# Attention steps of a fused two-block kernel: ScalarE's weight split behind the odd step's copy, TensorE's output-matrix products in front of the odd step's second turning

## The reference, cut to what matters

```
def attend_block(qi):                     # first_block, nsa_mixer
    s = einsum(q, k_cmp) - slope * d_cmp;  p_cmp = masked_softmax(s, d_cmp >= 0);  o_cmp = p_cmp @ v_cmp
    s = einsum(q, k_sel) - slope * d_sel;  p_sel = masked_softmax(s, d_sel >= 0);  o_sel = p_sel @ v_sel
    s = einsum(q, k_win) - slope * d_win;  p_win = masked_softmax(s, m_win);       o_win = p_win @ v_win
    return g[0] * o_cmp + g[1] * o_sel + g[2] * o_win
o = lax.map(attend_block, ...)            # all query blocks, [256, 16 * 64]
return o @ w_out                          # the output matrix, 1024 x 1024
```

## Time and profile before

| what | value |
|---|---|
| median of 3 runs | 2440.98 us (2439.84 to 2443.73) |
| profiled execution: own time | 2448.22 us |
| profiled execution: span of the trace | 2446.4 us |
| mean granted TensorE clock | 0.989 of full |
| PE busy | 2319.2 us (95%) |
| DVE busy | 1764.6 us (72%) |
| ACT busy | 1270.6 us (52%) |
| attention steps in the trace | about 838 to 926 us from the span's start |

### The profile page before, as it was taken

The page is one execution under the profiler, slowest core; times in us unless marked ns, Lnnn a source line. Parts: engine busy times, 40 slices in busy tenths (PEclk is TensorE's granted clock), DMA queues, the critical chain, the costliest instruction groups (busy, mean ns, idle before and its releaser), DMA issues.

```text
span 2446.4 us, 44735 instructions
## 1 busy us (share of the span) xinstructions
PE 2319.2 (95%) x16584; PEld 2055.4 (84%) x16584; DVE 1764.6 (72%) x2815; ACT 1270.6 (52%) x1939; POOL 12.2 (0%) x28
## 2 busy tenths in 40 slices
PE   4999999998999889999999999999999999999998
PEld 4888888888888768888889898888888888988887
DVE  6888978888888677766667575666666675746666
ACT  4445354453545565446446573554464475536544
POOL 0000000000000000000000000000000000000000
PEclk9999999999999999999999999999999999999999
DMA  8886868868898314754555341455555543404653
GB/s 322 303 290 217 292 249 295 291 218 294 301 308 302 104 53 163 240 199 156 191 190 177 129 139 55 155 174 190 190 174 191 189 164 122 147 30 155 200 191 123
DMA packets 130436, 481.39 MB, mean 197 GB/s; under 512 B 14608, under 2 KB 14656, under 8 KB 129776
## 3 DMA queue, kind: packets, MB, share of 16 engines
q1 hardware_dynamic: 128448, 468.36, 56.1%
q0 software_dynamic: 1840, 10.93, 1.2%
HBM read 478.15 MB, written 1.07 MB: 196 GB/s over the span
## 4 chain that ended last, share of the span: by engine, by line
PE 76%; DVE 9%; ACT 8%; issue 5%; DMA 2%; SPq 0%; DVEq 0%; ACTq 0%
PE bank L589 74%; ACT work L1367 2%; ACT w_hi L1367 2%; DMA ring<-weights 2%; DVE w_lo L1975 2%; ACT sq L1367 1%; DVE y L2009 1%; PE bank L620 1%; ACT L1367 1%; ACT h_split L1367 1%; PE bank L1183 0%; DVE work L2355 0%; DVE y L2487 0%; DVE work L2282 0%; DVE y L2123 0%
## 5 line engine op out<-in xcount | busy, mean ns | idle before, releaser
L589 PE MATMUL bank<-h_split,w_hi 128*128 128x256 f32 (+1 forms) x5232 | 1147.1, 341 | 27.2 <-DVE w_lo L1975 10.3
L1975 DVE TENSOR_TENSOR w_lo<-ring,w_hi 128x1024 fp32r<-128x1024 f32 x715 | 871.1, 1223 | 378.9 <-ACT w_hi L1367 378.1
L1367 ACT ACTIVATE w_hi<-ring 128x1024 fp32r<-128x1024 f32 x726 | 765.2, 1057 | 641.5 <-PE bank L589 565.9
L589 PEld LDWEIGHTS bank<-h_split,w_hi 128*128 128x128 f32 x5232 | 894.2, 193 | 124.1 <-issue 22.0
L589 PE MATMUL bank<-h_split,w_lo 128*128 128x256 f32 x3896 | 741.2, 284 | 0.0
L589 PEld LDWEIGHTS bank<-h_split,w_lo 128*128 128x128 f32 x3896 | 611.5, 192 | 25.0
L1367 ACT ACTIVATE work<-bank 128x512 f32<-128x512 f32 (+1 forms) x249 | 146.8, 593 | 322.1 <-PE bank L589 293.5
L589 PE MATMUL bank<-w_hi,act_hi 128*128 128x512 f32 x704 | 275.3, 391 | 0.0
L589 PE MATMUL bank<-w_lo,act_hi 128*128 128x512 f32 x704 | 274.9, 391 | 0.0
L589 PE MATMUL bank<-w_hi,act_lo 128*128 128x512 f32 x704 | 273.9, 389 | 0.0
L2009 DVE CUSTOM_DVE_ANT_0 y<-ring,v_first 128x1024 f32<-128x1024 f32 x160 | 189.6, 1220 | 14.6 <-DMA ring<-weights 14.6
(11 more groups left out here) (217 smaller groups left out, 1570.0 us busy)
## 6 DMA issues: line engine op xcount, KB each, us to landing
ring<-weights SPq DMA_DIRECT2D x886, 512.0 KB, 4.9
work<-cmp POOLq DMA_DIRECT2D x1, 4096.0 KB, 14.7
sq<-rows POOLq DMA_DIRECT2D x6, 512.0 KB, 6.2
work<-lora POOLq DMA_DIRECT2D x2, 1024.0 KB, 5.1
x<-x_in SPq DMA_DIRECT2D x1, 1024.0 KB, 11.1
out<-y SPq DMA_DIRECT2D x2, 512.0 KB, 2.6
const_sb<-consts SPq DMA_DIRECT2D x1, 854.0 KB, 12.7
const_sb<-consts POOLq DMA_DIRECT2D x1, 726.0 KB, 7.2
```

The costliest lines, as they stand in the source:

```text
L589: return nc.tensor.matmul(out, lhsT, rhs, start=start, stop=stop, skip_group_check=skip)
L1367: return nc.scalar.activation(out, in_, f, bias=bias, scale=scale, **kw)
L1975: tt(w_lo[q % SLOTS][:, :], ring[n % RING][:, c * HALF:(c + 1) * HALF], w_hi[q % SLOTS][:, :].bitcast(F32), ALU.subtract).then_inc(halves_ ...
```

## The change

Two edits in the loops over the 16 steps.

On TensorE, the odd step's second turning moves from in front of the previous step's output-matrix products to behind them. On ScalarE, the split of the next weight half (`advance`) moves from behind `exps(s+2)` in step 1 and the even steps 2 to 14, to between `copy(s)` and `exps(s+2)` in the odd steps 1 to 15. Step 0's split stays where it is. The halves split are the same and in the same order. VectorE's, GpSimd's and SyncE's programs are unchanged.

```
--- before.py
+++ after.py
@@ -907,8 +907,6 @@
                     turned_(s, 0)
                     if 0 < s < 14:
                         scores(s + 2)
-                    if s % 2:
-                        turned_(s, 1)
                     if s == 0:
                         pe.wait_ge(*at_vec.at("pc"))
                         for i in range(4):
@@ -917,6 +915,8 @@
                         ins.then_inc(*at_pe.step("cmp_turned"))
                     if s:
                         spread_half(s - 1)
+                    if s % 2:
+                        turned_(s, 1)
                     values(s)
                 spread_half(15)
@@ -1602,14 +1602,14 @@
                     if s:
                         high(s - 1)
                     copy(s)
+                    if s % 2:
+                        advance(st.half + 12 + s // 2)
                     if s < 14:
                         exps(s + 2)
                     if s == 14:
                         root_table()
-                    if s < 2:
-                        advance(st.half + 11 + s)
-                    elif s % 2 == 0:
-                        advance(st.half + 12 + s // 2)
+                    if s == 0:
+                        advance(st.half + 11)
                 high(15)
```

## The result

The changed kernel took 2452.19 us, the median of 6 executions (2450.44 to 2454.53), against 2442.69 us for 6 executions of the kernel before (2439.84 to 2446.42). The ratio is 1.0035, 95% interval 1.0025 to 1.0045: slower by 6 to 11 us. The forecast was 2445.5 us and its range ended at 2448.4. The direction was right and the size wrong: the two medians differ by 9.5 us, where 4.5 was forecast. Later samples say how much of the difference belongs to the change: two further sets of 12 executions of the same changed kernel gave ratios of 1.0016 and 1.0023, that is 4.0 and 6.2 us.

The account below looks back on a forecast made before the run. The prediction took the alternation of ScalarE and VectorE in the attention steps as the bound, with TensorE entering the path after the change. Terms 2.3 + 1.65 + 0.5 = 4.5 us on 2441.0 gave 2445.5 us, range 2442.6 to 2448.4.

Parts of the forecast that it names:

- What bounds the kernel: Attention steps: ScalarE and VectorE wait for each other in turn, 10.0 us per pair; TensorE is near this chain, not in it.
- The split costs nothing in its new place: ScalarE, odd steps: the moved split falls into idle time before the exponentials, so its 0.95 us per pair leaves the chain.
- The second turning: TensorE, odd steps 3 to 13: behind six products it makes VectorE's copy 0.39 us late per pair, 2.3 us in all.
- Step 1: First odd attention step: half-clock products make the copy 2.60 us late, the split gives back 0.95, so 1.65 us longer.
- the bound of 0.3: First odd attention step: 0.3 us more if TensorE's clock rises one turning later.
- rival of a full clock in step 1: TensorE runs the first odd step's products at full clock: term 0.41 us instead of 1.65, total 2444.2 us; chance 0.18.
- The end: Steps 14 and 15: no gain from the split, and the later turning makes `values(15)` 0.5 us late, bounds 0.3 and 0.7.
- The sum against the runs: Whole kernel: the terms' 4.5 us added to the 2441.0 us median of the runs shown, giving 2445.5 us.
- the rival with more half-clock time: Attention steps: one or two more clock dips, 1.24 us each, make it 6.4 us longer, 2447.4 us; chance 0.20.

## Why the prediction was right and wrong

**What bounds the kernel** (right). The ping-pong of `low`, `biased`, `exps`, `high`, with TensorE just off it. A pair of 10.00 us goes to 9.05 when ScalarE gives 0.95 back, and to 11.28 when TensorE's turning comes 1.28 later. Both were shown by single edits.

**The split costs nothing in its new place** (shown). Its relief of 0.95 us per pair is there in full, seven times.

**The second turning** (right, mis-sized by 0.06). The forecast had 10.39 us per pair, the trace has 10.33. The turning started 1.47 us behind the first of the six products in the pair shown, where I had taken the 1.59 from products followed by values. On the other side the products started 912.81 - 908.25 = 4.56 us behind `low(11)`, where the forecast had 908.77 - 904.28 = 4.49. Six times 0.06 is 0.3 us.

**Step 1** (right in its mechanism, a little small). I took 1.65 us; the three traces have 1.91, 1.68 and 1.68. The first has the turning at half clock too, 0.89 us instead of 0.60: the bound of 0.3 that I had put beside it. My rival of a full clock in step 1 held in none of these three traces; with the new order a full clock is seen only in the two traces with idle products.

**The end** (right). 0.56 us measured, 0.5 forecast.

**The sum against the runs** (the step that failed). I wrote "so I add it to the median: 2441.0 + 4.5". That median was of three executions, and 92 later ones of the same kernel have a median of 2444.2 and reach from 2438.9 to 2450.8. The base was 3.2 us low (1.7 against the 2442.69 of the six beside the changed kernel). I had seen that the profiled execution lay 7.2 us above it and called that a difference spread over the program; it was a sign of the scatter, and I gave the runs "some 2 us" of it when they had a standard deviation of 2.8. My range gave half clock a price only inside the attention steps, not in the rest of the program. The six executions that measured the change had a mean clock of 0.9877 against 0.9896 for the 92, worth 2.1 us by the slope above. So 2452.2 is 2444.2 for the kernel before, 4.2 for the change, 2.1 for the clock, and 1.7 that I cannot assign. The difference of 9.5 us has one part more: the six executions beside it had a median 1.5 us under that of the 92, which makes 4.2 + 2.1 + 1.7 + 1.5. The 2.1 rests on time and clock going together over the executions; no run sets the clock and measures the time. A range built on three executions should by my estimate have been some 4 us wider upward (twice the error of such a median at that deviation), and the rival with more half-clock time (2447.4 us) was nearer to the time measured than my forecast, though its place was wrong: the steady pairs kept a full clock in every trace.

**What stays open.** Whether the change itself makes TensorE's clock fall more often. The 30 executions of the changed kernel have a mean clock of 0.9887, those of before 0.9896: 1.0 us by the slope. That would raise the change's cost from 4.2 to 5.3 us (the difference of the means), and the three samples of the changed kernel, 0.9877, 0.9898 and 0.9881, differ as much among themselves. In step 1 all five traces with the second turning behind products and no idle ones had the half clock, and two of five with the old order. The Trainium skill (TensorE: Matmul & The Clock Gate, Part 1: The HAM clock gate) says that the gate's window runs freely. The traces agree so far as that the same instructions ran at another clock in another execution: the scores issued in step 1 started at 846.29 us and took 2.08 us at 0.50 in the first trace of the changed kernel; in the second they started at 847.67 and took 1.13 us, with a clock of 1.00 from 846 to 850.

## What to carry to other kernels

When two engines alternate, an engine "just off" their loop has no slack to give: before its order is changed, add up what the moved instruction will stand behind, from the point that releases it, and compare with the partner that was ready last. Here TensorE stood idle for 1.15 us ahead of the turning, and for 0.21 us with ScalarE's edit alone. Putting 1.5 us of products there cost 1.3 us per pair. Two edits that touch different engines should be timed apart: by the traces one was worth -6.6 us, the other +11.1. And a forecast is given on the level of many executions, not of three.

## What the runs showed of the hardware that I had not expected

One program of identical instructions scattered over 12 us (2438.9 to 2450.8 in 92 executions), and its mean granted clock went with it, 1.1 us per 0.001. In the rows of the changed kernel, transposes started earlier behind six products of 512 columns than values did: 1.47 us behind the start of the first product, where the values had 1.58. Sixteen records of idle products, 8 calls with 128 columns, took 2.05 us at full clock. The clock of the same TensorE instructions in step 1 was half in two traces and full in three, so one trace doesn't tell where it falls.
